# The last two levels of the delta rule's inversion: 32x32 products in tiles of the array, turns and products issued by turns

## The reference, cut to what matters

```python
a = jnp.where(strict, jnp.einsum('bhnid,bhnjd->bhnij', k_beta, k) * decay, 0.0)
eye = jnp.eye(CHUNK, dtype=a.dtype)
rhs = jnp.concatenate([v * beta[..., None], k_beta * jnp.exp(cum)[..., None]], axis=-1)
sol = lax.linalg.triangular_solve(a + eye, rhs, left_side=True, lower=True, unit_diagonal=True)
...
def step(state, xs):
    u_c, w_c, q_c, k_c, attn_c, last_c = xs
    v_new = u_c - jnp.einsum('bhck,bhkv->bhcv', w_c, state)
    o = jnp.einsum('bhck,bhkv->bhcv', q_c, state) + jnp.einsum('bhij,bhjv->bhiv', attn_c, v_new)
    state = state * last_c[..., None, None] + jnp.einsum('bhck,bhcv->bhkv', k_c, v_new)
```

## Time and profile before

| | |
|---|---|
| median of 3 runs | 1894.73 us (1892.38 to 1896.58) |
| the profiled execution, its own time | 1893.11 us |
| its span, first to last instruction | 1891.3 us |
| mean granted TensorE clock | 0.986 of full speed |
| busy: PE, PEld | 1828.7 us (97%), 1666.7 us (88%) |
| busy: DVE, ACT, POOL | 1261.5 us (67%), 972.9 us (51%), 108.3 us (6%) |
| busy in 332.2 to 485.0 us, `gdn_back`'s 16 units: PE, DVE, ACT | 148.2, 121.9, 104.4 us |

### The profile page before, as it was taken

One profiled execution on the slowest core, in us unless ns is written; L12 is line 12 of the kernel. 1 busy time (PEld: TensorE's weight loads), 2 busy tenths in 40 slices (PEclk: granted clock), 3 DMA queues, 4 the chain that ended last, 5 costly groups with the idle time before them and its releaser, 6 DMA issues. The chain is left out here.

```text
span 1891.3 us, 33607 instructions
## 1 busy us (share of the span) xinstructions
PE 1828.7 (97%) x13026; PEld 1666.7 (88%) x13026; DVE 1261.5 (67%) x2243; ACT 972.9 (51%) x1803; POOL 108.3 (6%) x142
## 2 busy tenths in 40 slices
PE   7999999999899999999999999999999998999998
PEld 7999999799689999999999977788899985787776
DVE  6666789986752977777655276597777757863444
ACT  6557764567741844444444257374444433424662
POOL 0001141000000000000000020000000002000101
PEclk9999999999999999999999999999999998999999
DMA  8223472245342233233232232223223232321101
GB/s 206 73 91 108 130 202 53 74 137 168 111 106 68 79 108 106 89 94 106 90 91 77 61 100 80 89 90 112 90 89 111 90 111 69 112 68 45 45 23 45
DMA packets 209652, 179.61 MB, mean 95 GB/s; under 512 B 42544, under 2 KB 181808, under 8 KB 209512
## 3 DMA queue, kind: packets, MB, share of 16 engines
q1 hardware_dynamic: 209512, 177.68, 31.8%
HBM read 164.10 MB, written 13.54 MB: 94 GB/s over the span
## 5 line engine op out<-in xcount | busy, mean ns | idle before, releaser
L196 PE MATMUL ps<-ffn_alo,main_whi 128*128 128x264 f32 (+1 forms) x768 | 205.7, 322 | 0.0
L196 PE MATMUL ps<-ffn_ahi,main_wlo 128*128 128x264 f32 (+1 forms) x768 | 205.1, 321 | 0.0
L196 PE MATMUL ps<-ffn_ahi,main_whi 128*128 128x264 f32 (+1 forms) x768 | 204.7, 321 | 0.0
L196 PE MATMUL ps<-gdn_xhi,gdnf_whi 128*128 128x264 f32 x768 | 160.5, 290 | 4.2 <-DVE gdnf_wlo L1551 4.2
L499 DVE TENSOR_TENSOR main_wlo<-raw,main_whi 128x512 fp32r<-128x512 f32 x212 | 144.9, 685 | 21.0 <-ACT main_whi L389 11.4
L196 PE MATMUL ps<-gdn_xlo,gdnf_whi 128*128 128x264 f32 x768 | 156.1, 284 | 0.0
L196 PE MATMUL ps<-gdn_xhi,gdnf_wlo 128*128 128x264 f32 x768 | 156.0, 284 | 0.0
L561 DVE TENSOR_TENSOR h<-h,ps 128x528 f32<-128x528 f32 (+1 forms) x128 | 88.9, 695 | 88.2 <-PE ps L196 87.6
L165 DVE TENSOR_TENSOR main_wlo<-raw,main_whi 128x2048 fp32r<-128x2048 f32 x38 | 88.1, 2319 | 79.7 <-ACT main_whi L158 79.7
L196 PEld LDWEIGHTS ps<-ffn_ahi,main_whi 128*128 128x128 f32 x768 | 127.8, 188 | 11.2
L196 PEld LDWEIGHTS ps<-ffn_alo,main_whi 128*128 128x128 f32 x768 | 127.5, 188 | 11.0
(11 more groups left out here) (553 smaller groups left out, 4850.9 us busy)
## 6 DMA issues: line engine op xcount, KB each, us to landing
raw<-in_ff_up_dram SPq DMA_DIRECT2D x32, 1024.0 KB, 5.5
raw<-in_ff_down_dram SPq DMA_DIRECT2D x32, 1024.0 KB, 5.0
raw<-in_gdn_in_dram SPq DMA_DIRECT2D x24, 1024.0 KB, 5.6
raw<-in_w_in_dram SPq DMA_DIRECT2D x14, 1024.0 KB, 5.3
raw<-in_mlstm_in_dram SPq DMA_DIRECT2D x12, 1024.0 KB, 5.3
raw<-in_gdn_out_dram SPq DMA_DIRECT2D x8, 1024.0 KB, 6.4
gdn_zr<-gdn_z_spilled SPq DMA_DIRECT2D x26, 264.0 KB, 3.0
gdn_v_spilled<-gdn_o SPq DMA_DIRECT2D x16, 264.0 KB, 2.3
```

The source lines that it names most:

```text
L196: mm = pe.matmul(ps[:, b, 0:k.width], w, x[:, half], start=first and n == 0, stop=last and n == 2)
```

## The change

In `open5` and `close5` each head's product, 96 columns wide, becomes two products of 32x32 with 32 moving columns, one for each pair of blocks (`b` = 0 and 1). In `open5` they read partitions 32 to 63 and 96 to 127, in `close5` 0 to 31 and 64 to 95; both write partitions 0 to 31 and 64 to 95 of the bank that was written before. `z5` is 32 columns a head instead of 64, and ACT's copy of it and the reads of `corner5` follow. In `open6` each head's transpose is followed by the same head's product, where all four transposes stood ahead of all four products; the transposes now write `flat[6]` and the products `flat[7]`. The waits, the order of the blocks and the other engines' work are as before.

```diff
-        xb5, yb5 = flat[6].rearrange("p (h n) -> p h n", h=GRP), flat[6][:, 0:GRP * 64]
-        zb5, xzb6, yb6 = flat[7][:, 0:GRP * 64], flat[7].rearrange("p (b n) -> p b n", b=2), flat[7][:, 0:GRP * 64]
+        by_head = lambda t: t[:, 0:GRP * BLK].rearrange("p (h n) -> p h n", h=GRP)
+        xb5, yb5, zb5, zs5 = flat[6].rearrange("p (h n) -> p h n", h=GRP), by_head(flat[6]), by_head(flat[7]), by_head(z5)
+        xzb6, yb6 = k.ps[3][:, :, 0:GRP * 64], flat[7][:, 0:GRP * 64]
+        corner = lambda b: slice(64 * b, 64 * b + BLK)
+        later = lambda b: slice(64 * b + BLK, 64 * b + 64)
...
                 for h in range(GRP):
-                    y = yt[:, GRP * u + h, :].rearrange("p (b w) -> p b w", w=64)[:, :, 32:64]
-                    mm = pe.matmul(zb5[0:96, 64 * h:64 * h + 64], an[:, GRP * u + h, 0:96], y, start=True, stop=True)
+                    for b in range(2):
+                        mm = pe.matmul(zb5[corner(b), h, :], an[later(b), GRP * u + h, corner(b)],
+                                       yt[later(b), GRP * u + h, later(b)], start=True, stop=True)
                 mm.then_inc(s.z5_ready, 1)
...
                 for h in range(GRP):
-                    mm = pe.matmul(yb5[0:96, 64 * h:64 * h + 64], x5[0:96, h, 0:96], z5[0:96, 64 * h:64 * h + 64],
-                                   start=True, stop=True)
+                    for b in range(2):
+                        mm = pe.matmul(yb5[corner(b), h, :], x5[corner(b), h, corner(b)], zs5[corner(b), h, :],
+                                       start=True, stop=True)
                 mm.then_inc(s.y5_ready, 1)
             def open6(u):
                 pe.wait_ge(s.y5_done, 2 * u + 2)
                 for h in range(GRP):
                     pe.transpose(xzb6[0:64, 0, 64 * h:64 * h + 64], yt[0:64, GRP * u + h, 0:64], k.ident[0:64, 0:64])
-                for h in range(GRP):
                     mm = pe.matmul(xzb6[0:64, 1, 64 * h:64 * h + 64], an[64:128, GRP * u + h, 0:64],
                                    yt[64:128, GRP * u + h, 64:128], start=True, stop=True)
                 mm.then_inc(s.xz6_ready, 1)
...
-                nc.scalar.copy(z5[0:96, :], zb5[0:96, :]).then_inc(s.z5_done, 1)
+                nc.scalar.copy(zs5[0:96], zb5[0:96]).then_inc(s.z5_done, 1)
...
                     nc.scalar.copy(yt[p, head(u), 64 * r + 32:64 * r + 64],
-                                    yb5[p, :].rearrange("p (h b w) -> p h b w", h=GRP, b=2)[:, :, r, :])\
+                                    yb5[p])\
```

## The result

The changed kernel takes 1908.13 us (median of 6 runs, 1903.42 to 1910.54), the kernel before 1892.63 us (6 runs, 1891.63 to 1896.58): 15.5 us more by the medians, where 6.6 had been forecast. The ratio over all runs is 1.0077, 95% interval 1.0066 to 1.0088, which is 14.6 us (12.5 to 16.7).

The account below looks back on a forecast made before the run. PE, busy for 97% of the span, was taken to bound the kernel. Loss 0.77 less gain 0.29 gives 0.48 us a unit; 15 x 0.48 - 0.58 = +6.6 us, so 1901.3 us, range 1888 to 1910.

Parts of the forecast that it names:

- The drain at every swap: In `open6`, PE drains at every swap between 64x64 transpose and product; the block takes 1.71 us, loss 0.77 a unit.
- The 32x32 products: In `open5` and `close5`, a head's two products run side by side; 0.56 us a block, gain 0.29 a unit.
- rival B: 32x32 products writing one bank from different rows each drain: 1933 us, or 1917 with free swaps; chance 0.14, both forms.
- rival C: In `open5` and `close5`, 32x32 products run one behind another, losing 0.21 us a unit: 1909 us; chance 0.09.
- The steady slot: Slots 9 to 11, one pass of `step` each, take 9.7 us instead of 9.2.
- The covers and waits: `new_values` covers copy `z5`; `close6`'s cover holds in steady slots, not slots 0 to 2; slot 8's 1.1 us wait swallows slot 7's share.
- The sum: Each unit of `gdn_back` takes 0.48 us longer; 15 pass it on, less 0.58 us: +6.6 us.
- The range: Total time 1888 to 1910 us, leaving out rival B; the forecast alone runs from 1899 to 1908 us.

Follow-up runs that it names:

- the turns alone: Kernel before with only `open6` changed: transposes and products alternate over two banks, level 5 products stay 96 wide; 1903.17 us, ratio 1.0059.
- two banks: Kernel before with the 32x32 products, and all `open6` transposes, writing `flat[6]`, ahead of all products, writing `flat[7]`; 1891.24 us, ratio 1.0004.
- plain turns: Changed kernel with the 64x64 transposes of `open6` made by ordinary fp32 products with the identity; 1889.97 us, ratio 0.9986 against the kernel before.
- the filler: Changed kernel with four unread full-width fp32 products between `open6` and `close6` in slots 1 and 2; 1904.99 us, ratio 1.0084 against the kernel before.

## Why the prediction was right, and where not

- **The drain at every swap, +0.77 us a unit: right.** `open6` from the first turn (435.76) to the first update took 1.71 us, 1.71 forecast; the turns alone make a slot 9.99 us, 0.77 more. That it is the form and not the bank, argued from the earlier trace rows, was shown twice: two banks keep the drain, plain turns remove it.
- **The 32x32 products, -0.29 us a unit: right.** A slot with them alone is 0.28 shorter. Pair pace 0.031 us, as forecast. Neither rival B (one bank, two row groups) nor rival C (one behind another) was there. By the Trainium skill (TensorEngine Tiling, Gotcha 1: PSUM Pressure) different row tiles cannot access the same bank at the same time. Here two row tiles write one bank, in different partitions of it, and start as a pair, at 0.031 us a pair; the measurement decides.
- **The steady slot, 9.7 us: right**, 9.71 in slots 4 to 6 and 9 to 11.
- **The covers and waits: right.** `close6` waits only in the first slots (2.0 us, 2.3 in the earlier trace rows), slot 8's wait for `put_back` shrank from 1.1 to 0.6 us, and the stall at 463 us is gone. The prediction has `new_values` cover the copy `z5` and does not say that slot 1 has no such block: there PE waits 0.5 us for it, but it waited 0.6 us before, so this moved nothing. PE's list:

```profile
PE ps L2334 <- ACT gdns_xz L2426: 2.0, 3, 0.7
PE ps L2306 <- DVE raw L1924: 0.6, 1, 0.6
PE ps L2321 <- ACT gdns_z L2421: 0.5, 1, 0.5
```

- **The sum, 15 x 0.48 - 0.58 = +6.6 us: short by 9 us.** The step that failed is the last one: it multiplied a steady slot's difference by 15 and took the granted clock of slots 0 to 3 as that of before, though the difference was measured at full clock, and though those are the slots in which PE is not full. The change's own work is some 6 us, by the kernel with the changed form from slot 4 on and by the fast runs with the filler. The rest, some 9 us in the median run, lies in the first slots: in the profiled execution, 17.4 us slower than that of before, slots 1 to 3 alone took 13.3 us more (38.4 less 25.1 us).
- **The range: held, by luck.** The prediction gave the forecast's own range as 1899 to 1908; the median of 1908.13 lies at its edge because of a term that the range did not hold. It also lies next to the 1909 of rival C, whose mechanism the trace refutes: the time alone would have spoken for the wrong cause, and only the slots tell them apart. The direction was forecast rightly, and for the right reason.

What stays open is why the pair of edits keeps the clock low so much more than either alone. Shown are the place (slots 0 to 3) and the pair (7 us; for either edit alone 1 to 2 us beyond its own work, which the runs don't separate from none), and that more work in the idle time of slots 1 and 2 does not settle it. In these slots the pair has the shortest products, the most drains and a PE that still waits for others; which of these the chip answers to, the runs don't tell.

## What to carry to other kernels

Before products are interleaved with turns, look in the trace at the load behind a swap: if it starts after the matmul ahead of it has streamed and not beside it, every swap costs that gap, and a small transpose that sits among small fp32 products may be better made as a product with the identity, twice the records and no drain. That was measured for 64x64 alone; the full-width turns of the kernel before (L2241) have no idle time ahead of their loads. A loss or gain worked out in a slot at full clock should be carried only to slots at full clock: list the windows with the granted clock beside the busy time, and give the stretches that are only partly busy a term of their own, since there a change of form can cost more than its work, or save nothing because another engine is caught up with. When two edits are worth +11.1 and -1.3 us alone and +15.5 together, switch them by stretch: where the sum comes apart is where the third cause lies. And look for every rival in the slots and not in the total, which here stood next to the number of a wrong one.

## What the runs showed of the hardware

- 64x64 fp32 turns and 64x64 fp32 products on different rows of the array do not run side by side (0.43 us for one turn and one product of two records); two 64x64 fp32 products there do, starting 0.01 us apart.
- 32x32 fp32 products on two row groups run side by side though they write one PSUM bank, in different partitions: 16 records start in pairs within 0.22 us.
- The granted clock depended on the combination of two edits: medians of the clock over the runs were 0.987 with the turns alone, 0.986 with the 32x32 products alone, 0.981 with both (0.979 to 0.984).
- The same kernel, with four more products in two slots, ran at 1897 us or at 1905 to 1920 us, in step with its mean clock.
